# Final norm of an MoE layer spread over five of the last six expert steps, with five sets of touched rows gathered in the last

## The reference

```
def hier_moe(h, w_rg, b_rg, w_re, b_re, w_eg, w_eu, w_ed):
    ...                                   # top-1 of 4 groups, top-2 of its 8 experts, a gate for each
    y = routed_experts(t, expert, w_eg, w_eu, w_ed)
    return jnp.einsum('nk,nkd->nd', gate.astype(t.dtype), y).reshape(B, T, D)
...
        return (jax.nn.silu(xb @ w_eg[e]) * (xb @ w_eu[e])) @ w_ed[e]
...
    x = x + hier_moe(rms_norm(x, g_ffn), w_rg, b_rg, w_re, b_re, w_eg, w_eu, w_ed)
...
    y_prompt = rms_norm(xp, g_final)
    y_sample = rms_norm(xs, g_final)
```

## Time and profile before

| what | value |
| --- | --- |
| median of 3 runs | 2546.25 us (2544.87 to 2548.96) |
| profiled execution | 2547.73 us |
| its span in the trace | 2545.9 us |
| busy: PE, DVE, ACT, POOL | 2442.2, 873.4, 475.6, 503.1 us |
| transfers over the span | 394.13 MB, 155 GB/s in the mean |
| scatters (L1561) | 42, one for each step |
| one set or tile: square of 1024 columns on ACT | 1.03 us, and 0.19 us for its sum |
| DVE's add (one or two terms), DVE's scale | 0.15 or 0.21 us, 1.28 us |
| POOL's power alone | 0.55 to 0.6 us |

### The profile page before, as it was taken

One profiled execution on the slowest core, in us unless ns is written; L12 is line 12 of the kernel. 1 busy time (PEld: TensorE's weight loads), 2 busy tenths in 40 slices (PEclk: granted clock), 3 DMA queues, 4 the chain that ended last, 5 costly groups with the idle time before them and its releaser, 6 DMA issues.

```text
span 2545.9 us, 29792 instructions
## 1 busy us (share of the span) xinstructions
PE 2442.2 (96%) x9503; PEld 1118.8 (44%) x9504; DVE 873.4 (34%) x2395; ACT 475.6 (19%) x984; POOL 503.1 (20%) x613
## 2 busy tenths in 40 slices
PE   8999999999999997999999998999999999999984
PEld 4444444444444664555555553333333333333331
DVE  1586757657585202233333333011111111111123
ACT  2222222122111123222222211010100010100023
POOL 1122222222223000011111112221122221222223
PEclk9999999999999999999999999999999999999997
DMA  6212111111143317322121127947697479797996
GB/s 229 104 36 58 38 62 38 42 54 38 55 169 131 134 46 277 132 66 67 67 67 67 59 78 257 315 143 233 216 322 223 126 228 325 235 322 224 332 350 227
DMA packets 154957, 394.13 MB, mean 155 GB/s; under 512 B 20782, under 2 KB 21318, under 8 KB 154859
## 3 DMA queue, kind: packets, MB, share of 16 engines
q1 hardware_dynamic: 130354, 327.81, 36.4%
q0 software_dynamic: 19712, 47.87, 7.7%
q10 hardware_dynamic: 4800, 17.32, 1.7%
HBM read 324.62 MB, written 69.12 MB: 155 GB/s over the span
## 4 chain that ended last, share of the span: by engine, by line
PE 56%; DMA 2%; issue 1%; DVE 1%; POOL 1%; ACT 0%; POOLq 0%; ACTq 0%; SPq 0%; DVEq 0%
PE r_pss L2185 21%; PE r_psx L2185 11%; PE r_psx L2149 9%; PE r_pss L2122 9%; PE r_pst L2174 2%; PE r_psr L2158 1%; DMA W<-in_w_expert_up 1%; PE r_pst L2141 1%; PE r_psr L2196 1%; PE r_pss L2186 1%; PE r_pst L2114 1%; PE r_pst L2131 1%; DMA f_acc<-x_scratch 0%; PE r_psk L2196 0%; DMA out_y_p<-f_acc 0%
## 5 line engine op out<-in xcount | busy, mean ns | idle before, releaser
L2185 PE MATMUL r_pss<-W,r_h2T 128*64 x1312 | 574.7, 596 | 9.8 <-DMA W<-in_w_expert_gate 5.7
L2186 PE MATMUL r_pss<-W,r_h2T 128*64 128x512 f32 x1312 | 574.7, 596 | 0.0
L754 PE MATMUL a_psz<-W 128*128 128x512 f32 x1088 | 481.1, 595 | 1.3 <-ACT W L512 1.3
L607 DVE SCALAR_TENSOR_TENSOR yacc<-aext,pcol,yacc 128x256 f32<-128x256 f32 x928 | 370.9, 477 | 0.3 <-issue 0.3
L2185 PEld LDWEIGHTS r_pss<-W,r_h2T 128*64 128x64 f32 x1312 | 180.5, 138 | 382.2 <-issue 382.2
L754 PEld LDWEIGHTS a_psz<-W 128*128 128x128 f32 x1088 | 203.5, 191 | 237.5 <-issue 237.5
L2185 PE MATMUL r_psx<-W,r_x1r 128*64 x656 | 290.1, 595 | 2.3 <-issue 0.2
L2186 PE MATMUL r_psx<-W,r_x1r 128*64 128x512 f32 x656 | 290.3, 595 | 0.0
L2149 PE MATMUL r_psx<-W 128*128 128x512 f32 x544 | 237.4, 594 | 0.0
L2122 PE MATMUL r_pss<-W,r_h2T 128*128 128x512 f32 x512 | 226.9, 596 | 3.1 <-POOL r_tokens L1490 3.1
L1959 DVE TENSOR_TENSOR r_x1r<-r_pss,r_x1r 128x256 f32<-128x256 f32 x84 | 31.8, 420 | 500.1 <-PE r_pss L2186 474.0
(11 more groups left out here) (366 smaller groups left out, 2264.8 us busy)
## 6 DMA issues: line engine op xcount, KB each, us to landing
W<-in_w_expert_gate SPq DMA_DIRECT2D x32, 2048.0 KB, 10.9
W<-in_w_expert_up SPq DMA_DIRECT2D x32, 2048.0 KB, 9.9
W<-in_w_expert_down SPq DMA_DIRECT2D x32, 2048.0 KB
W<-in_x_prompt SPq DMA_DIRECT2D x32, 512.0 KB, 4.1
x_scratch<-W SPq DMA_DIRECT2D x18, 512.0 KB, 3.0
r_x1r<-x_scratch SPq DMA_DIRECT2D x18, 512.0 KB, 4.4
x_scratch<-r_x SPq DMA_DIRECT2D x17, 512.0 KB, 2.9
h_scratch<-r_h SPq DMA_DIRECT2D x17, 512.0 KB, 2.9
```

The source lines that it names most:

```text
L607: ins = dve.scalar_tensor_tensor(out=out, in0=src, scalar=w, in1=yacc[:, i, :], op0=ALU.mult, op1=ALU.add)
L754: last = pe.matmul(psz[bank][:], hT[t.par][:, k, :], w_in[bank][:, k, :], start=(k == 0), stop=(k == KD - 1))
L2185: pe.matmul(out[0:HALF, :], xt[:, 0:HALF], W[:, bass.ds(base + at, 512)], start=start, stop=stop)
L2186: return pe.matmul(out[HALF:P, :], xt[:, HALF:P], W[:, at:at + 512], start=start, stop=stop)
```

## The change

LAST goes from 4 to 6: steps 36 to 41 are now the ones in line, with j = 0 to 5, and the loop ends one pair earlier. The 16 tiles are spread over them by a table, `ROUNDS = (2, 3, 3, 4, 4, 0)`, and tile n uses buffer n % 4. So steps 36 to 40 load 2, 3, 3, 4 and 4 tiles, and step 41 none; step 41 stores the four tiles of step 40. A load still waits for the store that had its buffer before. There are six sets of touched rows. Five are gathered in step 41 ahead of the last scatter, the fourth into `yb[0]` and the fifth into `acc[0]`, as soon as the last tile of that buffer is stored. Behind the last scatter POOL writes the first two sets before it gathers the rows of step 41, and the other three after. The squares of the sets on ACT come behind its last y and no longer between stores.

```diff
-LAST = 4
-ROUND = 4
+LAST = 6
+RING = 4
+ROUNDS = (2, 3, 3, 4, 4, 0)
...
+def tiles_of(j):
+
+    if j < 0:
+        return range(0)
+    return range(sum(ROUNDS[:j]), sum(ROUNDS[:j + 1]))
...
-            redo = [x1n[0][:], x1n[1][:]] + [x[:].rearrange("p k n -> p (k n)") for x in xT]
+            redo = [x1n[0][:], x1n[1][:], xT[0][:].rearrange("p k n -> p (k n)"), yb[0][:], acc[0], xT[1][:].rearrange("p k n -> p (k n)")]
...
                         fetch_again(t)
-                        if 0 <= j < LAST - 1:
-                            for i in range(ROUND - 1):
-                                final_rstd(ROUND * j + i)
+                        tiles = tiles_of(j)
+                        for n in tiles[:-1]:
+                            final_rstd(n)
                         if j == LAST - 1:
...
+                            pool.wait_ge(F["redo_known"], 2 * j)
                             for m in range(LAST - 1):
+                                if m == 4:
+                                    pool.wait_ge(acc_out[0], 16 * (PT // RING))
                                 gather_redo(m)
                             for m in range(LAST - 1):
                                 pool.wait_ge(redo_here[m], 16)
                         if j >= 0:
                             pool.wait_ge(F["redo_known"], 2 * j + 2)
-                            for i in range(ROUND):
-                                pool.wait_ge(acc_here[i], 16 * (j + 1))
+                        for n in tiles:
+                            pool.wait_ge(acc_here[n % RING], 16 * (n // RING + 1))
                         scatter(t)
...
                     expert_steps(pool, pairs, work)
-                    for i in range(ROUND):
-                        final_rstd(ROUND * (LAST - 1) + i)
                     final_rstd(PT)
                     final_rstd(PT + 1)
+                    for i in range(RING):
+                        pool.wait_ge(acc_out[i], 16 * (PT // RING))
+                    scatter_redo(0, PT)
+                    final_rstd(PT + 2)
+                    scatter_redo(1, PT + 1)
+                    final_rstd(PT + 3)
...
                     gather_redo(LAST - 1)
-                    final_rstd(PT + 2)
-                    final_rstd(PT + 3)
-                    for i in range(ROUND):
-                        pool.wait_ge(acc_out[i], 16 * LAST)
-                    for m in range(LAST - 1):
+                    final_rstd(PT + 4)
+                    for m in range(2, LAST - 1):
                         scatter_redo(m, PT + m)
+                    final_rstd(PT + LAST - 1)
                     final_rstd(PT + LAST)
                     scatter_redo(LAST - 1, PT + LAST)
...
                    def final_load(j):
-                        for i in range(ROUND):
-                            need(act, acc_out[i], 16 * j)
-                            act.dma_start(acc[i], x2_d[2 + ROUND * j + i, :, :]).then_inc(acc_here[i], 16)
+                        for n in tiles_of(j):
+                            need(act, acc_out[n % RING], 16 * (n // RING))
+                            act.dma_start(acc[n % RING], x2_d[2 + n, :, :]).then_inc(acc_here[n % RING], 16)
...
                    def work(t, j=-LAST):
...
-                        if j >= 0:
+                        if tiles_of(j):
                             final_load(j)
                         y_evac(t)
                         if j >= 0:
                             final_squares(j)
                     expert_steps(act, pairs, work)
-                    final_store(LAST - 1)
+                    for m in range(LAST - 1):
+                        act.wait_ge(redo_here[m], 16)
+                        square_whole(PT + m, redo[m])
```

39 lines of the change are left out of this document (19 added, 20 removed).

## The result

| | before | after |
| --- | --- | --- |
| median | 2546.35 us (2544.87 to 2548.96, 19 runs) | 2551.7 us (2548.52 to 2557.7, 19 runs) |
| span of the profiled execution | 2545.9 us | 2552.2 us |
| ratio of the times | | 1.002, 95% interval 1.0013 to 1.0027 |

The kernel before was run again beside the changed one, and its median of 19 runs is 2546.35 us. The change makes the kernel slower by 5.35 us (3.3 to 6.9 by the interval), where the forecast was 1.8 us slower (2548.0) and its range ended at 2554. The time lies in the range, but 0.7 us outside the 2544 to 2551 that the prediction kept for the forecast itself. It lies also at the border between "the same" and "slower", which the prediction put at 5.1 us.

What follows compares the result with a forecast made beforehand. The experts run at PE's pace with the DMA engines close behind; the end is something else. A of +6 us and B of -4.2 us gave +1.8 us, so 2548.0 us on the median of 2546.25, range 2540 to 2554.

Steps and rivals of the forecast that it cites:

- A: PE's waits for weights in steps 38 to 41: +6 us, bounds -8 to +13, from tile traffic ahead of the last weights.
- A, step 39: Gate weights for step 39 land at 2441.9, 6.7 us late; with 1.6 us of slow clock the step costs 8.3 more.
- What twelve transfers take less what the idle time absorbs: Ahead of step 39's gate weights: 12 tile transfers of 1.3 us, 15.6 us, less 6.0 us of idle DMA time.
- the 3.9 us for the place where the loop is left: Leaving the loop before step 36 issues the weights of steps 36 and 37, and everything behind them, 3.9 us later.
- A, step 40: Step 40 cost 8.1 us before; it would now cost 6, bounded from 0 to 8.1.
- Rival 2: Late weights compound, step 40 waits as long as before: A 9.6 to 11, sum +7, 2553 us; chance 0.18.
- B: What follows PE's last product, the tail: -4.2 us, from -8.4 to +0.9.
- B, the last scatter: Last scatter waits for five gathers and no tile loads, going out at 2515.5: gain 1.5 us, from -1.9 to +4.4.
- B, behind the scatter: Last scatter to end: gather 0.6 us sooner, three writes hidden in its flight, delay 2.6 falls to 0.5; gain 2.7 us.
- Rival 3: Tail gives nothing: gathers land as late as loads, early writes delay the last gather; B -0.5, 2551.7 us; chance 0.10.
- three signs of being wrong: Step 39's weights in time; a chain over tile loads behind step 41; PE waiting for gathered rows or y.
- six of being right: Step 39 wait 4-9 us; step 40 under 6.5; DMA full; PE's end 4-8 later; scatter within 5; about 26 to end.

Runs made afterwards that it cites:

- e2: The changed kernel without the five final-norm tiles of steps 36 and 37 (those rows not computed): 2543.42 us, ratio 0.9993.
- e8: The changed kernel with the tiles spread 0, 4, 4, 4, 4, 0 over steps 36 to 41: 2555.61 us, ratio 1.0035.
- e1: The changed kernel with the tiles back in the last four steps (0, 0, 4, 4, 4, 4) and a reordered tail: 2554.40 us, ratio 1.0029.
- e9: The changed kernel with DVE's last three scalings of gathered rows over 8 columns instead of 1024: 2549.95 us, ratio 1.0007.
- e10: The changed kernel with the final norm's gain copied to PSUM and read there by the scalings of gathered rows and the sample: 2548.83 us.
- e5: The changed kernel with only its tail reordered, last gather and last powers ahead of some writes, last sum before the sample's scaling: 2549.29 us, ratio 1.0012.
- e7: The changed kernel without POOL's writes of redone rows 2, 3 and 4: 2550.39 us.
- e11: The changed kernel with both the reordered tail and the gain read from PSUM: 2549.14 us, ratio 1.0007.
- e6: The changed kernel with tiles 2, 2, 0, 4, 4, 4, so step 38 has none, and a reordered tail: 2552.28 us, ratio 1.002.
- e13: The kernel before with only the gain read from PSUM in the scalings behind the loop: 2547.31 us, ratio 1.0002.

## Why the prediction was right or wrong

**What bounds the kernel.** Right: the chain of after goes over weights, then over the last scatter and POOL, and where PE starts again decides.

**A, step 39.** The mechanism was right: a wait at the gate product for weights that tiles held up, full DMA engines from step 37 on, and none of it if the early tiles are gone (e2). The size was too small. Forecast was a landing at 2441.9 and +8.3 us; it was 2444.6, a wait of 9.81 and, from one gate issue to the next, 34.45 us against 22.63, so +11.8, which leaves 2.0 for the slow clock (forecast 1.6).

Two terms of the landing were off, in opposite directions. What twelve transfers take less what the idle time absorbs, 15.6 - 6.0 = 9.6, came to 15.3 us (24.7 in after against 9.4 in e2). It took twelve tile transfers as standing ahead of the weights, and priced them at 415 GB/s. In after eight are issued ahead, and five behind, among them all three loads of step 38 (2430.16 on), which delay the weights too, as e8's stores do; and the engines moved 294 to 409 GB/s at a full share in the stretches above. The other term is the 3.9 us for the place where the loop is left. The weights of step 36 are indeed issued 4.3 us later (2374.82 against 2370.51), but e1 and e2, which leave the loop at the same place, have the gate weights for step 39 after 10.7 and 9.4 us, 2.1 and 0.8 more than before, and no wait. So it is by luck that the landing was missed by only 2.7 us.

**A, step 40.** 2.84 us of wait, and some 4.5 with the slow clock (products start 0.86 us apart instead of 0.43 behind it), where the forecast took 6, near its upper end. Measured from the gate issue for step 40 to DVE's last half of y it is 64.77 us against 68.47, -3.7, where the forecast had -2.1. That is why A is +8.15 (11.8 - 3.7) and not 11.8 - 2.1 = +9.7. Rival 2, in which late weights compound so that step 40 waits as long as before, had its condition met (over 8 us at step 39), and the time it gives for A, 9.6 to 11, did not come, since step 40 waits less.

**B, the last scatter.** Right: 1.77 us sooner, forecast 1.5. The fifth gather, issued at 2514.44, landed after 7.80 us at 2522.2, and the scatter goes out 1.2 us behind that, as the step said.

**B, behind the scatter.** Wrong: 0.1 instead of 2.7. The step said that the gather goes out 0.6 us sooner, and that three writes of 1.3 us fit into its flight. It did go out at 9.33 us, not 8.8, and the gather and two of the writes, which stand beside DVE's scalings, last 2.02 us and not 1.0. So the sample's power, its scaling and, behind that, the last set's sum are late, and the last set's power comes at 2542.18, 2.8 us behind the end of its squares (2539.39), as far behind as before. The durations were taken from rows of before in which POOL stood alone. The sign that wasn't used is in the same trace: beside scalings the gather lasts 1.26 us, one write 1.77 and two powers 2.04. e9 and e10 give 3.0 and 3.2 us when that is gone, which is the missing term (25.6 us measured in e10, about 26 forecast).

**Rival 3.** It gave 2551.7, the measured median, and that is luck. It had A at +6 and B at -0.5, and they came at +8.15 and -1.9. Its gathers should have landed as late as the loads did, and the scatter went out 1.77 us sooner; of its reasons only the early writes that push the last gather back are in the rows (e5 moves one of them and a power away, and the gather goes out at 7.2 us instead of 9.3).

**The sum.** +6 - 4.2 = +1.8 was forecast; +8.15 - 1.9 = +6.3 came in the profiled executions, +5.35 in the medians. The profiled executions are 2.4 and 1.4 us above their medians, hence the 1 us between the two. A was 2.15 too small, and B's gain was 2.3 too large: both made the forecast too fast. The time is in the range because the range was wide enough to take in rival 2. None of the three signs of being wrong came. Of the six of being right three came (2.84 us of waits in step 40, full DMA engines, the scatter 4.27 us behind y), and three did not: the wait at step 39 was 9.81 us and not 4 to 9, y came 8.15 us later and not 4 to 8, and from the scatter to the end it was 28.8 us and not about 26.

**Still open:** why after spreads over 9 us (before over 4). The waits at step 39 differ little from one profiled execution to the next (9.3 to 9.8 us in after, e5, e7, e9, e10 and e11), while the start of y's last half differs by 3.2 us. The start of step 36 differs by 3.4 us already, but the two don't go together: after starts it first of the six and takes longest from there to y, 153.5 us against 149.6 to 151.9.

## What to carry to other kernels

Price a transfer that is moved into a busy stretch by what all queues move until the awaited one lands, those issued later too, at the rate that the full stretch shows, and look in the awaited transfer's own queue for the backlog. A price for each transfer doesn't carry over: against e2 the ten of after cost 15.3 us, the eight of e8, moved in later, 15.5, and the eight of e6, moved in earlier, 9.0. Of an instruction on POOL take two durations from the trace, alone and beside a DVE instruction with two SBUF inputs; if it is the second that counts, put one of DVE's inputs in PSUM. A tile taken out of the last step saves only if what takes its place in the tail (sets to gather, powers, writes) is shorter than its own load and norm.

## What the hardware showed that was not expected

- POOL's issue of an indirect DMA lasts 2.02 us instead of 1.0, and a power on 128 numbers up to 1.5 instead of 0.57 (2416.76 in after), when a DVE instruction of 1.28 us with two SBUF inputs has started ahead of it. With one of the inputs in PSUM both go on side by side, at unchanged 1.28 us for DVE (e10, and for the powers e13).
- Stores of 0.5 MB issued 0.5 to 4.7 us behind a weight transfer of 2 MB on another queue landed 7 to 17 us ahead of it (e8).
- At a full share the 16 DMA engines moved between 294 and 409 GB/s in the stretches of 4 us shown from after, so a full share isn't one rate.
- The idle time of PE where the loop is left is 2.3 us before step 38 and 3.03 to 3.10 us before step 36, in every kernel that leaves it there.
- The length of a wait doesn't tell whether PE's clock falls. After 2.84 us at step 40 of after the products start 0.86 us apart and the granted clock from 2472 to 2476 is 0.60; after 3.58 us at step 39 of e6, and 2.87 and 2.93 us at step 40 of e2, they start 0.43 us apart from the second on, at a granted clock of 1.00.
